# Gate and up products in steps of 512 features with the tokens as TensorE's weights, in a fp32 transformer kernel on one core

## Chip, core and metric

One Trainium2 chip, one of its cores, everything in fp32. The time of a kernel is the device time of one execution in microseconds; each run gives the time of the core. The profile is that of one more execution, which has its own time.

## What is computed

256 tokens of width 1024 go through two stacks of two layers. The first stack has, in each layer, a gated feed-forward part (ffn), an attention mixer, a cross attention to 256 memory rows, and a second ffn. The second stack has in each layer a hybrid mixer (three kinds of attention, one of them "differential") and after it, in layer 0, a dense ffn, in layer 1 eight experts. The parts that the change touches:

```python
def swiglu_ffn(x, w_gu, w_down):                    # 1024 -> 2 x 2816 -> 1024, 5 times
    gate, up = jnp.split(x @ w_gu, 2, axis=-1)
    return (jax.nn.silu(gate) * up) @ w_down
# first stack, 4 of the 5: x + 0.5 * swiglu_ffn(rms_norm(x, gain), w_gu, w_down)
# second stack, layer 0:   h = rms_norm_2(x, g_ffn) * (1 + sc2) + sh2; x + gt2 * swiglu(h, ...)
# diff_attention, per head, two softmax maps p[0], p[1] of 32-wide halves:
a = p[:, :, 0] - lam * p[:, :, 1]
y = jnp.einsum('bhqs,bshd->bqhd', a, v)             # then rms_norm, gain
# moe_swiglu: for each of 8 experts, out += combine[e] * swiglu(h, w_gate[e], w_up[e], w_down[e])
```

## The kernel before

The program is one hand-written stream of instructions for each engine; semaphores alone order the engines among one another, and every wait is written out. A plan lists the stages (norm, ffn, mixer, ...) with the running counts of every semaphore, so that each engine's code can wait for "the n-th of this kind". The feature-major activations `xT` are eight tiles of 128 features x 256 tokens.

**Weights** come through a ring of 7 slots of 1 MiB (128 x 2048 fp32), filled by SyncE (SP) in the order of use. Before each load SP waits for the semaphore value that the plan noted in `released` for that slot's last reader (`slot_free`). SP's stream is in order, so that a load that waits holds back all behind it. Gate and up weights are two loads to a step of 256 features (`L790` gate, `L793` up), each of 1 MiB.

**An ffn** takes its 2816 features in 11 steps of 256 (`j`). Step 0 is the plain product (`gate_up`, `L1250`, `L1253`). Steps 1 to 10 are Winograd's form of Strassen's product: gate and up as the two column halves, the 1024 inputs as two halves, seven products M1 to M7 in the order M1, M5, M6, M2, M3, M7, M4 instead of eight (`products`, `L1293`). A piece of weights of 128x128 is TensorE's stationary operand and 128 token columns move; one step is 112 matmul records, the results lie feature-major, 128 features x tokens. VectorE forms the sums of weights S1 to S4 of the next step in pieces of 128x512 (`weight_sums`, `L2981` to `L2989`) and the sums of products U2, U3, C12, C21, C22 (`L3037`, `L3089` to `L3114`); ScalarE copies M1, M5, C11 out of PSUM and takes tanh for silu; VectorE multiplies gate by up (`L2995`, `L2997`: a "gated pair") into `hidden`. M4 of step j is issued behind M1 of step j+1. The down product (2816 to 1024) uses the same scheme from `hidden` as it lies (`down`, `L1344`; `down_sums`, `L3021` to `L3032`).

Between the products PE does small pieces for VectorE in its last bank (`through_last_bank`, `L1313`, `L1317`), for the modulation vector whose weights POOL loads and VectorE multiplies (`ada_part`, `L2915`).

**Norm ahead of an ffn:** PE transposes x (`L1118`), VectorE writes `xT` with the gain; 1/rms per token (`rs`) is needed feature-major along the tokens, so VectorE writes a diagonal, PE multiplies it by ones (`L1136`), and VectorE multiplies the result into `xT` (`L2545`). `keep_busy` (`L1108`) are matmuls without a use, placed where PE waits.

**Hybrid mixer:** of its pairs of heads the first `ROW_PAIRS` = 4 are differential. Both maps are transposed (3 transposes a block pair each) and both multiplied by v (`L1985`, 12 records); `turn_diff` (`L1948`) transposes the finished heads at pair i=5; `turn_weights` (`L1963`) waits for the scaled maps of its pair (`p_scaled`, VectorE `L2682`).

**Experts:** their gate and up weights (`L822`, `L823`, half a MiB each, one slot together) and down weights (`L826`) go through a ring of 7 + `MORE` = 10 slots in `EXPERT_ORDER`; PE's products are `L1439` and `L1482`. Extra slots lie in buffers of earlier stages, so SP waits for `wo_done` or the like ahead of their first use.

## Time and profile before

| | us |
|---|---|
| three runs of the kernel | 2682.12, 2683.52, 2688.59 (median 2683.52) |
| the profiled execution | 2680.09 |
| its span (first to last instruction) | 2678.3 |
| PE busy | 2560.3 (96%) |
| VectorE (DVE) busy | 1311.5 (49%) |
| ScalarE (ACT) busy | 435.4 (16%) |
| GpSimd (POOL) busy | 204.2 (8%) |

Matmuls overlap their neighbours in the pipeline, so a busy PE is not a PE at its peak; how long a piece of PE's work takes is read as the distance between the starts of its first row and of the next piece's. A fp32 matmul of the code shows as two records in the counts of the trace.

### The profile page before, as it was taken

Reading aid. Unit: us, or ns where it says so; the run is one execution under the profiler, and the core shown is the slowest. Engines: PE = TensorE matmul, PEld = TensorE weight load, DVE = VectorE, ACT = ScalarE, POOL = GpSimd, SP = SyncE. Lnnn points to the kernel's source line nnn. Section 1 sums busy time; section 2 is a strip of 40 time slices with the busy share of each in tenths; the row PEclk is TensorE's granted clock in tenths of the full one; section 3 lists DMA queues with packets and bytes.
Section 4 is the critical chain, followed back from the end, with each engine's and each line's share of the span. In section 5 each row is a group of like instructions: output and inputs, shape, how many; then the busy total and the mean of one; then the engine's idle time right before and its main releaser. Section 6 shows DMA issues by size and latency. Waiting matters only on the chain.

```text
span 2678.3 us, 44222 instructions
## 1 busy us (share of the span) xinstructions
PE 2560.3 (96%) x18150; PEld 1643.6 (61%) x18150; DVE 1311.5 (49%) x2784; ACT 435.4 (16%) x1187; POOL 204.2 (8%) x330
## 2 busy tenths in 40 slices
PE   8999999999999998999999999999999899989996
PEld 8964457797599444477964649945545344634452
DVE  6887442488877955425887556664630000101002
ACT  1201252011012013321101221102310110101010
POOL 3010100000000102000001110001100000000000
PEclk9999999999999999999999999999999999999999
DMA  9684323367656743234675434544359999999997
GB/s 299 205 318 160 110 95 126 117 216 255 214 189 220 252 157 126 82 108 152 217 254 150 136 115 154 186 160 119 113 224 403 412 413 412 417 412 411 409 417 311
DMA packets 306523, 619.18 MB, mean 231 GB/s; under 512 B 15948, under 2 KB 172784, under 8 KB 306192
## 3 DMA queue, kind: packets, MB, share of 16 engines
q1 hardware_dynamic: 287088, 550.80, 55.5%
q0 software_dynamic: 19232, 65.52, 7.3%
q8 instruction: 146, 2.39, 0.3%
q14 instruction: 57, 0.47, 0.0%
HBM read 607.47 MB, written 8.79 MB: 230 GB/s over the span
## 4 chain that ended last, share of the span: by engine, by line
PE 69%; issue 10%; DVE 9%; DMA 6%; SPq 4%; ACT 1%; POOL 1%; DVEq 0%; POOLq 0%; ACTq 0%
PE psum L1293 22%; PE psum L1439 10%; PE psum L1859 6%; PE psum L1482 5%; PE psum L1344 4%; PE psum L1574 3%; DMA xn<-in_w_ada 2%; PE psum L1209 2%; PE psum L1161 2%; PE psum L1770 2%; DMA ring<-in_w_exp_up 2%; PE psum L1880 2%; SPq L822 2%; SPq L823 2%; DVE proj L2915 1%
## 5 line engine op out<-in xcount | busy, mean ns | idle before, releaser
L1439 PE MATMUL psum<-ring,xT 128*32 128x512 f32 (+3 forms) x3372 | 293.0, 494 | 17.3 <-DMA ring<-in_w_exp_up 16.7
L3409 DVE SCALAR_TENSOR_TENSOR proj<-proj,psum 128x256 f32<-128x256 f32 (+1 forms) x63 | 24.9, 395 | 555.1 <-ACT proj L2326 555.1
L1439 PEld LDWEIGHTS psum<-ring,xT 128*32 128x32 f32 x3372 | 128.0, 110 | 168.4 <-issue 111.7
L1293 PE MATMUL psum<-xT,ring 128*128 128x128 f32 x1600 | 195.0, 275 | 0.0
L1293 PEld LDWEIGHTS psum<-xT,ring 128*128 128x128 f32 x1600 | 187.7, 192 | 4.1 <-issue 3.8
L1859 PE MATMUL psum<-ring,xT 128*128 128x384 f32 (+1 forms) x448 | 156.2, 498 | 1.1 <-DVE xT L2550 1.1
L2915 DVE SCALAR_TENSOR_TENSOR proj<-xn,cols,proj 128x512 f32<-128x512 f32 x168 | 126.0, 750 | 18.3 <-DMA xn<-in_w_ada 14.3
L1574 PE MATMUL psum<-ring,memT 128*128 128x512 f32 x256 | 119.3, 605 | 8.2 <-issue 8.1
L943 POOL DMA_DIRECT2D xn<-in_w_ada x96 | 69.5, 726 | 677.0 <-DVE proj L2915 670.4
L1859 PEld LDWEIGHTS psum<-ring,xT 128*128 128x128 f32 x448 | 80.9, 190 | 61.2 <-issue 10.8
L1161 PE MATMUL psum<-ring,y 128*128 128x512 f32 x256 | 113.5, 601 | 0.7 <-ACT kTx L2086 0.7
L1482 PE MATMUL psum<-ring,proj 128*32 128x256 f32 x1872 | 104.5, 379 | 0.0
L1344 PE MATMUL psum<-ring,proj 128*128 128x512 f32 x220 | 102.6, 592 | 0.0
L1293 PE MATMUL psum<-qT,ring 128*128 128x128 f32 x800 | 98.0, 276 | 1.4 <-DVE picked L3109 1.4
L1293 PE MATMUL psum<-diff_o,ring 128*128 128x128 f32 x800 | 97.5, 275 | 0.0
L1293 PEld LDWEIGHTS psum<-qT,ring 128*128 128x128 f32 x800 | 93.3, 192 | 5.6 <-DVE picked L3109 5.6
L1293 PEld LDWEIGHTS psum<-diff_o,ring 128*128 128x128 f32 x800 | 93.3, 192 | 0.0
L1482 PEld LDWEIGHTS psum<-ring,proj 128*32 128x32 f32 x1872 | 72.9, 110 | 32.4 <-issue 6.0
L2219 ACT ACTIVATE silu<-pT 128x256 f32<-128x256 f32 x100 | 41.9, 419 | 293.1 <-DVE pT L3037 185.1
L1161 PEld LDWEIGHTS psum<-ring,y 128*128 128x128 f32 x256 | 48.6, 192 | 59.0 <-issue 57.9
L1574 PEld LDWEIGHTS psum<-ring,memT 128*128 128x128 f32 x256 | 46.1, 192 | 59.0 <-issue 58.6
L2326 ACT ACTIVATE proj<-psum 128x256 f32<-128x256 f32 (+1 forms) x63 | 23.1, 367 | 345.4 <-PE psum L1439 345.4
(528 smaller groups left out, 4197.9 us busy)
## 6 DMA issues: line engine op xcount, KB each, us to landing
ring<-in_ffn_w_gu SPq DMA_DIRECT2D x88, 1024.0 KB, 7.3
ring<-in_w_exp_down SPq DMA_DIRECT2D x62, 1024.0 KB, 16.9
xn<-in_w_ada POOLq DMA_DIRECT2D x96, 512.0 KB, 4.9
ring<-in_ffn_w_down SPq DMA_DIRECT2D x44, 1024.0 KB, 7.4
ring<-in_w_exp_gate SPq DMA_DIRECT2D x82, 512.0 KB, 11.7
ring<-in_w_exp_up SPq DMA_DIRECT2D x82, 512.0 KB, 15.6
ring<-in_w_exp_gate SPq DMA_DIRECT2D x52, 384.0 KB, 9.8
ring<-in_w_exp_up SPq DMA_DIRECT2D x52, 384.0 KB, 12.4
```

What stands on the lines that cost most here:

```text
L822: sp.dma_start(slot(u)[:, 0:4 * w], g[rows, cut]).then_inc(full, 16)
L823: sp.dma_start(slot(u)[:, 4 * w:8 * w], up[rows, cut]).then_inc(full, 16)
L943: nc.gpsimd.dma_start(ada_slot[a % 2], wv[:, 2 * q:2 * q + 2, half * 3072 + c * 512:half * 3072 + (c + 1) * 512])\
L1161: ins = mm(banks[linear_bank(st, s, b)][:, 0:w], lhsT(k, b), wt[:, k - i * ks, :], start=(k == 0), stop=(k == KT - 1))
L1209: ins = mm(banks[bank][:, :], tokens[:, k, :], w[:, k, :], start=(new and k == 0), stop=(k == 3), skip_group_check=True)
L1293: ins = mm(banks[bank][:, t * P:(t + 1) * P], weights(t)[:, k, :], tokens[:, k, :], start=(new and t == 0 and k == 0), stop=(k == 3), skip ...
L1344: ins = mm(banks[bank][:, :], tokens, weights, start=(d == 0), stop=last, skip_group_check=True)
L1439: ins = mm(o[:, :, o0:o1], xg[e % 2][:, k, 32 * g:32 * g + 32], w_[:, :, c0:c1], start=(k == 0 and n_ == 0), stop=(k == KT - 1), skip_grou ...
L1482: ins = mm(bank[32 * g:32 * g + 32, at:at + 256], tokens[:, 32 * tg:32 * tg + 32], wt[:, f, d0:d0 + 256], start=first and at == 0, stop=la ...
L1574: ins = mm(banks[7][:, :], memT[:, k, b * P:(b + 1) * P], slot(u).rearrange("p (k n) -> p k n", k=4)[:, k % 4, :], start=(k == 0), stop=(k ...
L1859: ins = mm(banks[(5, 7)[b]][:, 0:w], xT[:, k, b * P:(b + 1) * P], slot(u)[:, 0:4 * w].rearrange("p (k n) -> p k n", k=4)[:, k % 4, :], sta ...
L2915: ins = V.scalar_tensor_tensor(ada_sum, w, cols[:, 16 + k:17 + k], ada_sum, ALU.mult, ALU.add)
```

## The change

- **Gate and up, all five ffns.** Step 0 becomes `gate_up_rows`: the weights are 128x128 tiles of tokens (`xT`), 512 weight columns (256 gate, 256 up) move. The other ten steps become five of 512 features (`w` = 1 to 5, `WIDE`), in the same seven products, with sums of tokens as stationary weights and 512 feature columns moving: 4 matmuls (8 records) of 512 columns a product. A quarter of a step's weights is a unit: A11, A21, A22, A12, in this order, each loaded by two transfers of half a MiB (`L825`). Each weight sum is one instruction of 128x2048; VectorE's order around them is new.
- The hidden values now come out token-major, so PE transposes them for the down product, four 128x128 transposes for 256 features (`turn_hidden`, `L1361`), and ScalarE copies them out.
- **Norm, the four ffns of the first stack** (`how="plain"`): rs is not multiplied into `xT`; gating takes it per token (tanh of rs/2 times gate, and rs squared in the second gating instruction, as a scalar per partition). The ones product and two `keep_busy` of two matmuls go.
- **Hybrid mixer:** VectorE combines the two maps before they are transposed; transposes and value products of the differential pairs halve; `turn_diff` moves to i=8 and loses its `keep_busy`.
- **Experts:** `MORE` is 6; the three added slots lie in the buffers `cst`, `qk_rows`, `sp_rows`, one further slot (`ONCE`) is used once in `xn`.

The core of the diff:

```diff
-MORE = 3
+MORE = 6
+EXPERT_ORDER = (0, 1, 2, RING, RING + 3, RING + 2, RING + 4, RING + 5, 3, 4, 5, 6, RING + 1)
...
-        add("norm", how="early", src="x", gain=("ffn1_norm", layer), dst="xT")
+        add("norm", how="plain", src="x", gain=("ffn1_norm", layer), dst="xT")
...
-            for j in range(NSTEP):
-                done = n["tiles"] // 2 + j + 1
-                released += [("gu_done1", done), ("gu_done1", done)]
+            released += [("gu_done1", t + 1)] * 2
+            for w in range(1, WIDE + 1):
+                done = t + 1 + 2 * w
+                released += [("gu_done0", done), ("product_done", n["products"] + 7 * w - 1), ("gu_done1", done), ("gu_done0", done)]
...
+                def gate_up_unit(u, j, half):
+                    rows = slot(u).rearrange("p (k t n) -> p k t n", k=4, t=2)
                     slot_free(sp, u)
-                    sp.dma_start(slot(u).rearrange("p (k n) -> p k n", k=KT), gv[:, :, cut])\
-                        .then_inc(slot_full(u), 16)
-                    slot_free(sp, u + 1)
-                    sp.dma_start(slot(u + 1).rearrange("p (k n) -> p k n", k=KT), uv[:, :, cut])\
-                        .then_inc(slot_full(u + 1), 16)
+                    for t, wv in enumerate((gv, uv)):
+                        sp.dma_start(rows[:, :, t, :], wv[:, 4 * half:4 * half + 4, j * FSTEP:(j + 1) * FSTEP]).then_inc(slot_full(u), 16)
+                u0 = st["n0"]["units"]
+                for half in range(2):
+                    gate_up_unit(u0 + half, 0, half)
+                for w in range(1, WIDE + 1):
+                    for name in UNITS:
+                        gate_up_unit(wide_unit(u0, w, name), 2 * w - (name[1] == "1"), int(name[2]) - 1)
...
...
+                    elif n == 12:
                         sp.wait_ge(sm["wo_done"], 8)
+                    elif n == ONCE:
+                        sp.wait_ge(sm["chosen_ready"], 1)
...
+                def gate_up_rows(b):
+                    if t0:
+                        pe.wait_ge(sm[f"hid_ready{b}"], t0)
                     for k in range(KT):
+                        if k % 4 == 0:
+                            unit_in(pe, u0 + k // 4)
+                        if b == 0:
                             ready(k)
+                        ins = mm(banks[4 + b][:, :], xT[:, k, b * P:(b + 1) * P],
+                                 slot(u0 + k // 4)[:, k % 4 * 512:(k % 4 + 1) * 512], start=(k == 0), stop=(k == KT - 1))
+                    ins.then_inc(sm[f"gu_done{b}"], 1)
...
+                    if name in ("M1", "M2"):
+                        unit_in(pe, wide_unit(u0, w, "A11" if name == "M1" else "A12"))
+                    elif term is not None:
+                        pe.wait_ge(sm["weights_summed"], weighed(n0, w, term))
+                    for k in range(4):
+                        ins = mm(banks[bank][:, :], tokens[:, k, :], weights[:, k * 512:(k + 1) * 512],
+                                 start=(new and k == 0), stop=(k == 3), skip_group_check=True)
+                    if name == "M3":
+                        ins.then_inc(sm["gu_done0"], 2)
+                    elif name == "M4":
+                        ins.then_inc(sm["gu_done1"], 2)
...
+                def turn_hidden(j):
...
+                    for f in range(2):
+                        for b in range(NB):
+                            ins = nc.tensor.transpose(banks[bank][:, (NB * f + b) * P:(NB * f + b + 1) * P],
+                                                      hidden_tile[2 * j + f][:, b * P:(b + 1) * P], ident)
+                    ins.then_inc(sm["product_done"], 1)
...
+                for w in range(1, WIDE + 1):
+                    products(w, "M1")
+                    if w > 1:
+                        products(w - 1, "M4")
+                        turn_hidden(2 * w - 3)
+                    through_last_bank(2 * w - 1, 0)
+                    products(w, "M5")
+                    through_last_bank(2 * w - 1, 1)
+                    products(w, "M6")
+                    products(w, "M2")
+                    through_last_bank(2 * w, 0)
+                    turn_hidden(2 * w - 2)
+                    products(w, "M3")
+                    through_last_bank(2 * w, 1)
+                    products(w, "M7")
+                turn_hidden(NSTEP - 2)
                 for d in range(NSTEP - 2):
+                    if d == LAST_TURN:
+                        turn_hidden(NSTEP - 1)
+                    if d == 0:
+                        down(0, "P2")
+                        products(WIDE, "M4")
                     for name in DOWN_PRODUCTS:
-                        down(d, name)
-                        if d == 0 and name == "P2":
-                            products(NSTEP - 1, "M4")
+                        if d or name != "P2":
+                            down(d, name)
...
                 def turn_diff():
-                    pe.wait_ge(sm["w2_evac0"], nb * (l + 1))
-                    keep_busy(5, 2)
...
-                        if i < ROW_PAIRS:
-                            pe.wait_ge(sm[f"p_ready{b}"], w + 1)
-                        else:
-                            pe.wait_ge(sm["p_scaled"], 2 * (n0["scaled"] + i - ROW_PAIRS) + b + 1)
+                        pe.wait_ge(sm["p_scaled"], 2 * (n0["scaled"] + i) + b + 1)
                         pe.wait_ge(sm[f"pt_evac{b}"], w)
-                        for h in range(2):
+                        for h in range(1 if i < ROW_PAIRS else 2):
...
+                elif st["how"] == "plain":
...
+                    V.tensor_scalar(half_rs, rs, 0.5, None, ALU.mult)
+                    V.tensor_tensor(square_rs, rs, rs, ALU.mult).then_inc(sm["diag_ready"], 1)
...
+                    if i < ROW_PAIRS:
+                        link(V.tensor_scalar(rden[:, :, 1], rden[:, :, 1], stat[:, 14:15], None, ALU.mult))
+                        for b in range(NB):
+                            p = p_sb[b][:, :, 0:(b + 1) * P]
+                            link(V.tensor_scalar(p[:, 0, :], p[:, 0, :], rden[:, b, 0:1], None, ALU.mult))
+                            V.scalar_tensor_tensor(p[:, 0, :], p[:, 1, :], rden[:, b, 1:2], p[:, 0, :], ALU.mult, ALU.add)\
+                                .then_inc(sm["p_scaled"], 1)
+                        return
...
+                            ins = V.tensor_tensor(S1, A21, A22, ALU.add)
...
+                            ins = V.tensor_tensor(S2, S1, A11, ALU.subtract)
+                        elif name == "S3":
+                            ins = V.tensor_tensor(A21, A11, A21, ALU.subtract)
+                        else:
+                            unit_in(dve, units["A12"])
+                            if w > 1:
+                                dve.wait_ge(sm["gu_done0"], t0 + 1 + 2 * (w - 1))
+                            dve.wait_ge(sm["weights_summed"], weighed(n0, w, "S2"))
+                            ins = V.tensor_tensor(S4, A12, S2, ALU.subtract)
+                        ins.then_inc(sm["weights_summed"], 1)
...
+                for w in range(1, WIDE + 1):
...
+                    if w > 1:
+                        second_column(w - 1, 1)
+                        last_sum(w - 1)
+                        second_column(w - 1, 0)
...
+                        ada_part(st, 2 * w - 1)
...
+                    V.tensor_tensor(c12_rows, banks[Z][:, :], m1_copy[w % 2], ALU.add).then_inc(sm["part_summed"], 1)
+                    if w < WIDE:
+                        weight_sums(w + 1, ("S1",))
+                    first_column(w, 0)
...
+                    if w < WIDE:
+                        weight_sums(w + 1, ("S2",))
...
+                    dve.wait_ge(sm["gu_done0"], t0 + 1 + 2 * w)
+                    V.tensor_tensor(c12_rows, banks[Y][:, :], c12_rows, ALU.add).then_inc(sm["part_summed"], 1)
+                    if w < WIDE:
+                        weight_sums(w + 1, ("S3", "S4"))
+                    else:
                         down_sums(0)
...
+                    first_column(w, 1)
+                    dve.wait_ge(sm["product_done"], produced(n0, w, "M7"))
+                    if w > 1:
+                        dve.wait_ge(sm["hid_ready1"], hidden_number(n0, w - 1, 1))
+                    V.tensor_tensor(second_rows, banks[Z][:, :], m1_copy[w % 2], ALU.add).then_inc(sm["part_summed"], 1)
+                    if "ada" in st:
+                        ada_part(st, 2 * w)
...
+                    V.tensor_tensor(second_rows, second_rows, m5_copy, ALU.add).then_inc(sm["part_summed"], 1)
```

In that code `c12_rows` is U2 and then C12, `second_rows` is U3 and then C22, `last_sum` is C21, `first_column` and `second_column` are the gated pairs (two instructions each), `from_last_bank` takes what `through_last_bank` made. The three places below show it in the streams.

**VectorE, one ffn step from U2 on, before.** (`kTx`, `s_sb`, `ring` hold weight sums, `picked` the token-side sums, `pT` values for gating, `proj` the hidden values.)

```order
L3089 TENSOR_TENSOR picked<-psum,kTt 128x256 [waits product_done,part_copied,part_summed]
L3037 TENSOR_TENSOR pT<-psum,picked 128x2x128 [waits gu_done1]
L2984 TENSOR_TENSOR kTx<-kTx,ring1 128x512 [waits weights_summed]
L2984 TENSOR_TENSOR kTx<-kTx,ring2 128x512 [waits weights_summed]
L2995 SCALAR_TENSOR_TENSOR silu1<-silu1,pT 128x256 [waits silu_done1,part_summed]
L2997 TENSOR_TENSOR proj<-pT,silu1 128x256 [waits gated1]
L3102 TENSOR_TENSOR pT<-psum,picked 128x2x128 [waits gu_done0,part_summed]
L2987 TENSOR_TENSOR s_sb0<-ring1,kTx 128x512 [waits weights_summed]
L2987 TENSOR_TENSOR s_sb1<-ring2,kTx 128x512 [waits weights_summed]
L2995 SCALAR_TENSOR_TENSOR silu0<-silu0,pT 128x256 [waits silu_done0,part_summed,part_copied]
L2997 TENSOR_TENSOR proj<-pT,silu0 128x256 [waits gated0]
L3109 TENSOR_TENSOR picked<-psum,kTt 128x256 [waits product_done]
```

VectorE in the changed kernel, first wide step of the first ffn, from `first_column(w, 0)` to U3:

```order
L3105 SCALAR_TENSOR_TENSOR silu0<-silu0,psum 128x256 [waits silu_done0]
L3108 SCALAR_TENSOR_TENSOR proj<-silu0,stat,psum 128x2x128 [waits gated0]
L3089 TENSOR_TENSOR vx<-kTx,ring3 128x2048 [waits weights_summed,product_done,ring_full3]
L3228 TENSOR_TENSOR pT<-psum,pT 128x512 [waits gu_done0,part_summed]
L3091 TENSOR_TENSOR ring4<-ring3,ring4 128x2048
L3097 TENSOR_TENSOR sp_rows<-ring6,vx 128x2048 [waits weights_summed,gu_done0,ring_full6]
L3105 SCALAR_TENSOR_TENSOR silu0<-silu0,pT 128x256 [waits silu_done0,part_summed]
L3108 SCALAR_TENSOR_TENSOR proj<-silu0,stat,pT 128x2x128 [waits gated0]
L3237 TENSOR_TENSOR hid<-psum,picked 128x512 [waits hid_ready1,product_done]
```

Before, no sum of weights between C12 (`L3102`) and U3 (`L3109`) waits for a slot of the ring; now S4 (`L3097`) does (`ring_full6`), and the second gated pair and U3 (`L3237`) stand behind it.

**SyncE, loads of gate and up, before** (a row is a transfer of 1 MiB; both loads of a step wait for the same count of M4):

```order
L790 DMA ring5<-in_ffn1_w_gu 128x8x256 [waits gu_done1]
L793 DMA ring6<-in_ffn1_w_gu 128x8x256 [waits gu_done1]
```

and in the changed kernel, the four units of one wide step, A11, A21, A22, A12:

```order
L825 DMA ring3<-in_ffn1_w_gu 128x4x256 [waits product_done]
L825 DMA ring3<-in_ffn1_w_gu 128x4x256
L825 DMA ring4<-in_ffn1_w_gu 128x4x256 [waits gu_done1]
L825 DMA ring4<-in_ffn1_w_gu 128x4x256
L825 DMA ring5<-in_ffn1_w_gu 128x4x256 [waits gu_done0]
L825 DMA ring5<-in_ffn1_w_gu 128x4x256
L825 DMA ring6<-in_ffn1_w_gu 128x4x256 [waits gu_done0]
L825 DMA ring6<-in_ffn1_w_gu 128x4x256
```

The plan gives A12 of step w+1 the slot of A11 of step w, and its load the wait for `gu_done0`, which counts M3 of step w.

**PE in the changed kernel**, M1 and M4 and then M2, a turn and so on (`x3` are further rows of the same form):

```order
L1335 MATMUL psum<-sp_rows,xT 128x512 [waits weights_summed,part_copied]
L1335 MATMUL psum<-sp_rows,xT 128x512 x3
L1335 MATMUL psum<-ring0,diff_o 128x512 [waits weights_summed,part_summed]
L1335 MATMUL psum<-ring0,diff_o 128x512 x3
L1335 MATMUL psum<-ring3,xT 128x512 [waits ring_full3,hid_ready0]
L1335 MATMUL psum<-ring3,xT 128x512 x3
L1335 MATMUL psum<-ring1,qk_rows 128x512 [waits part_summed]
L1335 MATMUL psum<-ring1,qk_rows 128x512 x3
L1361 MATMUL psum<-cst,proj 128x128 [waits part_copied,hid_ready0]
L1361 MATMUL psum<-cst,proj 128x128 x3
```

`ring3` begins M1 of step w+1, and M4 of step w (`ring1`) stands behind it with a wait for `part_summed`, the count that U3 of step w raises. Before, M4 of step j stood behind M1 of step j+1 with the same wait.

## Rows read from the trace of the kernel before

Rows of a timeline: start and length in us, engine, line, operation, out<-in, shapes, count, and in brackets how long the engine had been idle and what ended it. A row that bundles several matmuls ends a little after the next row starts.

**Rows 1.** The page: busy time of the engines; DMA share in 40 slices.

```profile
PE 2560.3 (96%) x18150; PEld 1643.6 (61%) x18150; DVE 1311.5 (49%) x2784; ACT 435.4 (16%) x1187; POOL 204.2 (8%) x330
...
DMA  9684323367656743234675434544359999999997
```

**Rows 2.** Chain that ended last, one Strassen step: start, us, what.

```profile
82.78 12.51 PE psum L1293 x112
95.28 0.44 PE psum L1313 x4
```

**Rows 3.** Timeline, PE, down product of 512 columns.

```profile
163.19 1.88 PE L1344 MATMUL psum<-kTx,s_sb 128*128 128x512 f32 x4
164.90 1.02 PE L1344 MATMUL psum<-ring,s_sb 128*128 128x512 f32 x2
```

**Rows 4.** Timeline, PE, norm, first step and first product of an ffn.

```profile
498.46 2.09 PE L1118 MATMUL psum<-cst,x 128*128 128x128 f32 x16
...
503.73 3.69 PE L1250 MATMUL psum<-xT,ring 128*128 128x256 f32 x16 [0.27 <-DVE xT L2545]
...
517.62 1.61 PE L1293 MATMUL psum<-xT,ring 128*128 128x128 f32 x13
```

**Rows 5.** Timeline, PE's last product of a step and the load that it releases.

```profile
44.23 1.95 PE L1293 MATMUL psum<-xT,ring 128*128 128x128 f32 x16
44.43 0.54 SPq L793 DMA_DIRECT2D ring<-in_ffn_w_gu  x1
```

**Rows 6.** The loads of `L793`, all of them.

```profile
DMA to landing us min/median/max: 5.0/5.2/13.7
```

**Rows 7.** DMA issues, SyncE, 1960.5 to 1961.3 us: KB each, us to landing.

```profile
ring<-in_w_exp_gate SPq DMA_DIRECT2D x1, 512.0 KB, 3.5
ring<-in_w_exp_up SPq DMA_DIRECT2D x1, 512.0 KB, 4.4
```

**Rows 8.** Groups of VectorE by form: busy us, mean ns, idle before.

```profile
L2989 DVE TENSOR_TENSOR ring<-ring 128x512 f32<-128x512 f32 x100 | 64.1, 682 | 0.0
L2997 DVE TENSOR_TENSOR proj<-pT,silu 128x256 f32<-128x256 f32 x100 | 42.5, 425 | 3.4
L3102 DVE TENSOR_TENSOR pT<-psum,picked 128x256 f32<-128x256 f32 x50 | 21.2, 423 | 53.2 <-PE psum L1293 53.2
```

**Rows 9.** Timeline, VectorE's `down_sums`, C12, and PE's M4 of the last step.

```profile
149.74 0.28 DVE L3021 TENSOR_TENSOR p_sb<-proj 128x128 f32<-128x128 f32 x1
...
152.96 0.41 DVE L3102 TENSOR_TENSOR pT<-psum,picked 128x256 f32<-128x256 f32 x1
...
155.29 2.05 PE L1293 MATMUL psum<-qT,ring 128*128 128x128 f32 x16 [0.29 <-DVE picked L3109]
```

**Rows 10.** Timeline, PE, norm of another stage, which uses no rs row.

```profile
228.40 1.15 PE L1118 MATMUL psum<-cst,x 128*128 128x128 f32 x8 [0.77 <-DVE x L3052]
230.28 1.10 PE L1209 MATMUL psum<-ring,xT 128*128 128x512 f32 x2 [0.74 <-DVE xT L2570]
```

**Rows 11.** Timeline, hybrid mixer: value products, `keep_busy`, `turn_diff`, scaled maps.

```profile
1498.95 1.45 PE L1985 MATMUL psum<-proj,pT 128*128 128x64 f32 x12
...
1545.81 1.88 PE L1108 MATMUL psum<-cst 128*128 128x512 f32 x4
1548.70 0.66 PE L1948 MATMUL psum<-cst,y 128*128 128x128 f32 x4 [1.00 <-DVE y L2715]
...
1548.77 1.03 DVE L2682 TENSOR_TENSOR p_sb<-p_sb,rden 128x256 f32<-128x256 f32 x2
```

**Rows 12.** Stretches in the experts and the end: us, engines' busy, PEclk, DMA share, GB/s.

```profile
2200.00:2300.00 100.00, 100.00 (x1416) 57.66 (x1411) 8.11 (x21) 11.46 (x32) 1.62 (x3) 1.00 1.03 413
2600.00:2678.00 78.00, 51.25 (x504) 18.12 (x496) 14.51 (x22) 5.66 (x17) 5.14 (x6) 0.94 0.81 328
```

**Rows 13.** Timeline, SyncE's expert loads, and PE late in the last expert.

```profile
1960.61 0.33 SPq L822 DMA_DIRECT2D ring<-in_w_exp_gate  x1
...
2616.30 1.92 PE L1439 MATMUL psum<-kTx,xT 128*32 128x512 f32 x16 [3.08 <-DMA kTx<-in_w_exp_up]
```

More of the change, by code:

```diff
@@ L257, in block1 @@
         xattn()
-        add("norm", how="early", src="x", gain=("ffn2_norm", layer), dst="xT")
+        add("norm", how="plain", src="x", gain=("ffn2_norm", layer), dst="xT")
         add("ffn", w=("ffn2", layer), out="half", ada=2 * layer + 1)
@@ L278, in make_plan @@
     add("final")
-    n = dict(products=0, copies=0, sums=0, weighed=0, norm=0, early=0, chunks=0, units=0, tiles=0, pieces=0, pairs=1, staged=1, soft=1, scaled=0, stick=1, xupd=0, prep=0,
+    n = dict(diag=0, products=0, copies=0, sums=0, weighed=0, norm=0, early=0, chunks=0, units=0, tiles=0, pieces=0, pairs=1, staged=1, soft=1, scaled=0, stick=1, xupd=0, prep=0,
              roots=0, squares=0)
@@ L300, in make_plan @@
             n["early"] += how == "early"
+            st["diag"] = n["diag"]
+            n["diag"] += how in ("early", "plain")
         st["root_of"] = root
@@ L504, in build @@
         shift_sum = lamv[:, 1, 0, 0:NEXP]
-        logits, first, second, count = (s_sb[0][:, 0, 16 * n:16 * n + 16].rearrange("p (b e) -> p b e", b=NB) for n in range(4))
-        sel = p_sb[0][:, :, 0:P]
-        selT = qT[:, 0, :]
+        routing = pT_rows[:, :, :, :].rearrange("p h b s -> p (h b s)")
+        sel = routing[:, 0:S].rearrange("p (b s) -> p b s", b=NB)
+        selT = routing[:, S:2 * S]
+        order_tmp = routing[:, 2 * S:3 * S]
+        logits, first, second, count, part = (routing[:, 3 * S + 16 * n:3 * S + 16 * n + 16].rearrange("p (b e) -> p b e", b=NB)
+                                              for n in range(5))
+        shift = routing[:, 3 * S + 80:3 * S + 80 + NEXP]
         mem = y
@@ new lines, in gate_up_rows, with products @@
+                    ins.then_inc(sm[f"gu_done{b}"], 1)
+                n0 = st["n0"]
+                def products(w, name):
+                    X, Y, Z = ((4, 6, 5), (1, 3, 2))[w % 2]
+                    whole = {part: slot(wide_unit(u0, w, part)) for part in UNITS}
+                    bank, new, weights, tokens = {
+                        "M1": (X, True, whole["A11"], B11), "M2": (X, False, whole["A12"], B21), "M5": (Y, True, S1, T1),
+                        "M3": (Y, False, S4, B22), "M6": (Z, True, S2, T2), "M7": (Z, False, whole["A21"], T3),
+                        "M4": (Z, False, whole["A22"], T4)}[name]
+                    if name in ("M1", "M6") and w == 2:
@@ L1283, in products @@
                     elif name == "M4":
[L1284 removed]
+                        pe.wait_ge(sm["part_summed"], summed(n0, w, "U3"))
                     term = {"M5": "S1", "M6": "S2", "M3": "S4", "M7": "S3"}.get(name)
[L1287 to L1294 removed]
@@ L2008, in hybrid @@
                         scores(i + 1)
+                    if i == DIFF_AT:
+                        turn_diff()
                     beside(i, 1)
```

563 lines of the change are left out of this document (282 added, 281 removed).

## The prediction, made before the changed kernel ran

> **What bounds the kernel now.** I read the page first. PE is busy 96% of the span, VectorE 49%, ScalarE 16%; in the 40 slices DMA is the full resource only in the last quarter [rows 1]. So up to about 1900 us a piece of PE's work is worth its whole length, and another engine's work costs something only where PE waits for it. From there on it is turned round: between 2200 and 2300 us the DMA share is 1.03 at 413 GB/s, and late in the last expert PE waits 3.08 us for weights [rows 12, 13]; there only bytes, or the time at which their transfers start, count. The chain of waits through a feed-forward step is then nothing but PE: 12.51 us for the 112 records of a step of 256 features, next piece at 95.28 [rows 2]. PE has no stall there to lose, so a gain must come from fewer or shorter matmuls, and any new stall is a loss in full.
>
> **Sum, term by term.** Against the profiled execution (2680.1 us, span 2678.3), which lies 3.4 us under the median of the runs shown.
>
> *1. Columns.* A step of 256 costs 12.51 us, two of them 25.02 [rows 2]. The new product moves 512 columns, the form of the down product, whose four records take from 163.19 to 164.90, 0.4275 us each [rows 3]. Seven products of 8 records are 23.94 us. Saved: 1.08 us a wide step, 25 such steps in five ffns: **-27.0**. The plain step 0 runs from 503.73 to 517.62, 13.89 us [rows 4]; 32 records of 0.4275 are 13.68: **-1.0** for five.
>
> *2. Transposes.* Four records of 128 columns take 0.44 us [rows 2]. Each of the 11 pieces of 256 hidden features now needs four of them on PE: 11 x 0.44 x 5 = **+24.2**. ScalarE's copies behind them have an engine with 84% idle, and no product waits for one directly. Terms 1 and 2 together are nearly nothing: what wide products save, the turned layout takes back.
>
> *3. The wait for S4.* This decides. The plan puts the unit A12 of step w+1 into the slot of A11 of step w, whose load waits for M3 of step w. VectorE's S4 of step w+1 reads A12, and behind it in VectorE's order stand the second gated pair and U3 of step w; M4 of step w on PE waits for U3. Count from the end of M3: the load is issued 0.20 us after the product that frees it (44.23 to 44.43 [rows 5]). A unit of 1 MiB that has its slot alone lands after 5.2 us in the median, 5.0 at best [rows 6]; as two halves issued one behind the other the nearest row is 0.37 + 4.4 = 4.8 (the second half is issued 0.37 behind the first) [rows 7, 13]. I take 5.2, because the modulation weights that POOL loads and units released just before share the rings in most ffns. S4 is 128x2048; the widest sum in the trace is 128x512 at 0.682 us, and 128x256 takes 0.423 [rows 8]. That slope gives 0.682 + 6 x 0.259 = 2.24; four times the 512 form would be 2.73. A gated pair is 2 x 0.43, U3 at 128x512 0.68 [rows 8]. Sum 0.20 + 5.2 + 2.24 + 0.86 + 0.68 = 9.18 us. PE meanwhile has M7 and M1 of the next step, 16 x 0.4275 = 6.84. M4 waits 2.34 us. Steps w = 1 to 4 of each ffn have a next step, so 20 such waits: **+46.8**. Bounds: landing 4.8 gives 1.94 and +39; S4 at 2.73 gives 2.83 and +57; nothing at all is rival A. A wait here is not made up later, since PE has no other stall that it could shorten.
>
> On the landing the Trainium skill, DMA: Bandwidth & Descriptors, section "Anatomy of one DMA — SWDGE (gpsimd) path", has a rule: about 2.0 us and then the bytes at 436 GB/s. For 1 MiB that is 4.4 us, an estimate by that page, where [rows 6] has 5.0 at least. By it the wait would be 1.5 us, the term +31 and the result about 2692 against the median. On S4, VectorE: DVE Perf Modes, section on the TRN2 errata, has (N+151)/0.96 ns for a fp32 sum, 2.29 us at 2048 columns, which the slope of the rows (2.24) comes near; it would add 1 us to the sum.
>
> *4. The end of the wide steps.* In the last one VectorE has C12, `down_sums(0)` and the first gated pair before `turn_hidden(9)` can run. `down_sums` takes from 149.74 to 152.96, 3.22 us [rows 9]; with C12 at 0.68, the pair at 0.86 and 0.2 of signalling 5.0 us, against one product M7 of 3.42: PE waits 1.6, where the last M4 waited 0.29 [rows 9]. **+6.5** for five ffns (0 to +10, if the order behind it absorbs it, or if `turn_hidden(9)` also waits for a copy).
>
> *5. Norm.* PE's transposes start at 498.46, take 2.09, and the first product starts at 503.73 [rows 4]: with the ones product and `keep_busy` in between. Without rs the first product needs only `xT` of the first feature tile, 0.74 us behind the transposes in the stage that has this form already [rows 10]: 498.46 + 2.09 + 0.74 = 501.29, 2.4 us sooner. The first ffn of all gains nothing, as its weights are still landing; three times 2.4: **-7.2**. The two small instructions that make rs/2 and its square lie on VectorE under the 13.7 us of step 0; if that cover were gone they would cost about 0.4 us a norm.
>
> *6. Hybrid mixer.* A differential pair loses 3 transposes (0.33 us by [rows 2]) and half of the value products (1.3 us between starts, 1.45 in [rows 11], so 0.65): 0.98 x 4 = 3.9 a layer. At `turn_diff`, `keep_busy` and a wait of 1.00 stand between 1545.81 and 1548.70, 2.7 us that go. But the scaled maps of pair 5 are ready at 1548.77 + 1.03 = 1549.80 only [rows 11], and `turn_weights(5)` now comes sooner and waits for them: 1.5 given back. 5.1 a layer, **-10.2** for two. VectorE's combination of the maps replaces the separate scaling; if it becomes what the early pairs wait for, the gain shrinks to -4; if nothing is given back, -14.
>
> *7. Experts.* From the first expert on DMA sets the pace. A unit of 1 MiB at 413 GB/s is 2.54 us [rows 12]. Three slots more let three more units be moved before PE's first expert product: 3 x 2.54 = **-7.6**. Bounds 0 (their buffers come free too late, or the ring was not what held the stream) and -10.2 with the slot in `xn`.
>
> Sum: -27.0 - 1.0 + 24.2 + 46.8 + 6.5 - 7.2 - 10.2 - 7.6 = **+24.5**, so 2704.6 by the profiled execution and **2708** against the median. A difference under 0.3% (8 us) can't be told from none.
>
> **Rivals.**
>
> *A, the unit is in time (the other side).* If A12 lands within 5.2 - 2.34 = 2.9 us of M3's end, S4 costs PE nothing, and the sum is 24.5 - 46.8 = -22.3: 2661 against the median, faster. For it: without the landing, the rest (0.20 of issue, S4, pair, U3, 4.0 us) fits well under 6.84. Against it: the fastest 1 MiB in the trace took 5.0, half a MiB alone 3.5 [rows 6, 7]. The point from which it decides: waits under 0.7 us each make the kernel faster by over 0.3%. Chance 0.13.
>
> *B, the landing is short but not short enough.* The two halves go over the rings together with nothing beside them, and the unit lands 4.0 to 4.5 us after its issue (half a MiB took 3.5 [rows 7], and another half MiB at 413 GB/s is 1.3 more [rows 12], from its own start 0.37 later). Waits of 1.1 to 1.6 us, +23 to +33 in place of 46.8, so 2684 to 2694. This is the rival that the DMA page above stands for. Chance 0.14, most of it within 0.3%.
>
> *C, the clock.* Where PE had 51.25 us busy of 78, its granted clock in the mean was 0.94, not 1.00 [rows 12], which is a part of the stretch at 1.2 GHz. If each of the 20 waits puts half a product behind it (four records, 1.7 us) at 1.2 GHz instead of 2.4, that adds 1.7 us each, +34: 2742. Against it: short waits of 0.3 to 1 us in [rows 4, 9, 11] are not seen in the clock of the page. Chance 0.06.
>
> *My forecast*, waits of 1.9 to 2.8 us and the joined changes near their sizes: 0.67. Its own range is 2696 to 2722: landing -8, S4 +10, joined changes 6 either way, taken together by squares on the low side about 12 and on the high side 14.
>
> **Numbers.** 2708. Leaving out A (0.13) and C (0.06) gives 2680 to 2726. Faster by over 0.3% (below 2675.5): A, and a little of B with larger joined gains, 0.15. Within 0.3%: most of B, 0.12. Slower: 0.73.
>
> **What would show it.** In the changed kernel's trace each M4 of w = 1 to 4 should stand behind an idle time of PE of about 2.3 us that ends with U3 on VectorE, and VectorE's S4 behind an idle time that ends with a DMA of the ring; seven products should take 24 us, a turn 0.44, S4 2.2 to 2.3. First product of an ffn 2.8 us after the first transpose. Experts: the first product sees more units landed, the end comes 7.6 us sooner against the start of the experts. Wrong it would be if the idle time ahead of M4 is below 1.2 us (then the change is no loss), if the turns hide in waits that are there anyway, or if products of 512 columns run at other than 0.43 us a record.

## The result, and the profile of the changed kernel

| | before | changed |
|---|---|---|
| median of the runs of this comparison, us | 2682.88 | 2729.84 |
| lowest to highest | 2682.12 to 2688.59 | 2725.39 to 2732.47 |
| ratio (95% interval) | | 1.0169 (1.0148 to 1.0189) |
| span of the profiled execution | 2678.3 | 2730.3 |

The changed kernel is 47 us slower, where 25 were forecast; 2729.84 lies 4 us above the range. The wait that was forecast is there, in its place and at its size; PE's clock behind it, which the sum had at nothing, is not as forecast.

The first lines of the changed kernel's page, the engines and three of its groups (count, busy us, mean ns, idle time before and what ended it):

```profile
PE 2561.2 (94%) x13902; PEld 1271.9 (47%) x13902; DVE 1297.8 (48%) x2391; ACT 438.8 (16%) x1142; POOL 204.3 (7%) x330
...
L1335 PE MATMUL psum<-ring,qk_rows 128*128 128x512 f32 x200 | 106.9, 684 | 47.7 <-DVE hid L3237 47.7
...
L1335 PE MATMUL psum<-ring,diff_o 128*128 128x512 f32 x200 | 90.0, 593 | 0.7 <-DVE pT L3218 0.7
...
L3097 DVE TENSOR_TENSOR sp_rows<-ring,vx 128x2048 f32<-128x2048 f32 x25 | 57.3, 2291 | 38.8 <-DMA ring<-in_ffn_w_gu 30.1
```

PE is busy for as long as before [rows 1], with a quarter fewer matmuls. `ring,qk_rows` is M4, `ring,diff_o` is M7, the same number of matmuls of the same shape. (In the listing of PE's stream ahead of the prediction the first two products are therefore M3, from `sp_rows`, and M7; M1 and M4 follow.) Two things are to be seen. Ahead of M4 PE idles 47.7 us in all, and what ends it is U3 (`L3237`); VectorE's S4 (`L3097`) in its turn waits for a load. And M4 itself is busy 106.9 us where M7 takes 90.0: the same work at a mean of 684 ns in place of 593.

The chain that ended last, between 74.6 and 88 us, goes through one such wait:

```profile
75.06 0.02 issue
75.08 0.37 SPq L825
75.45 0.04 issue
75.49 4.79 DMA ring<-in_ffn_w_gu
80.28 0.02 issue
80.31 0.03 DVE sp_rows L3097
80.34 2.17 issue
82.52 0.43 DVE silu L3105
...
83.37 0.69 DVE hid L3237
84.07 0.04 issue
84.11 3.70 PE psum L1335 x8
```

M3 ends at about 75.06, SyncE issues the load, it has landed at 80.28, S4 runs, then the gated pair, then U3, and M4 starts at 84.11: 9.05 us, where the prediction had 9.18. PE's own timeline behind two waits of the same length (start, length, and in brackets the idle time):

```profile
555.30 5.40 PE L1335 MATMUL psum<-ring,qk_rows 128*128 128x512 f32 x8 [2.09 <-DVE hid L3237]
560.53 0.60 PE L1361 MATMUL psum<-cst,proj 128*128 128x128 f32 x4
...
584.25 3.70 PE L1335 MATMUL psum<-ring,qk_rows 128*128 128x512 f32 x8 [2.08 <-DVE hid L3237]
```

The first M4 takes until the next piece starts at 560.53, 5.23 us, the second 3.54. The windows of the two (length, busy and counts of PE, weight load, VectorE, ScalarE, GpSimd, then PEclk, DMA share, GB/s) say why:

```profile
584.00:588.00 4.00, 3.75 (x10) 1.79 (x11) 3.13 (x7) 0.99 (x2) 0.72 (x1) 1.00 0.14 24
...
555.00:561.00 6.00, 5.70 (x13) 2.63 (x14) 3.52 (x7) 0.99 (x2) 0.72 (x1) 0.72 0.29 87
```

Granted clock 1.00 (2.4 GHz) behind one wait, and a mean of 0.72, so 1.2 GHz for about half of the stretch, behind the other. Over the whole execution:

```profile
core 0: 2730.3 us, clock 0.987
```

and before:

```profile
core 0: 2678.3 us, clock 0.995
```

Span times clock is 2694.8 against 2664.9: of the 52 us between the two profiled executions about 30 are work and waits at full clock, 22 are the clock. The stretches at 1.2 GHz in the two traces say where: none stands in an ffn before the change, ten do after it (nine behind an M4, one behind a turn that had waited 2.45 us), 1.7 us lost in each; the rest stands in other stages.

By the starts of the first rows of each stage on PE, in us:

| | before | changed | difference |
|---|---|---|---|
| first transposes to first product, four ffns of the first stack | 21.7 | 13.1 | -8.6 |
| five ffns, first product to the next stage | 1064.7 | 1137.4 | +72.7 |
| two hybrid mixers | 292.6 | 281.2 | -11.4 |
| experts, first transposes to the end of the span | 714.4 | 713.5 | -0.9 |
| all else | 584.9 | 585.1 | +0.2 |

### The profile page after: what moved, and what is told of

Its sections match the earlier page's. It is cut to its first block, busy times and chain, and to the rows that moved or that the text cites. A ratio compares the mean times of both kernels' runs of the same rounds, so it can differ in the third digit from the quotient of the medians.

```text
span 2730.3 us, 35231 instructions
## 1 busy us (share of the span) xinstructions
PE 2561.2 (94%) x13902; PEld 1271.9 (47%) x13902; DVE 1297.8 (48%) x2391; ACT 438.8 (16%) x1142; POOL 204.3 (7%) x330
## 4 chain that ended last, share of the span: by engine, by line
PE 68%; DVE 9%; issue 9%; DMA 8%; SPq 4%; POOL 1%; ACT 0%; DVEq 0%; POOLq 0%; ACTq 0%
PE psum L1335 16%; PE psum L1515 11%; PE psum L1410 6%; PE psum L1935 6%; PE psum L1558 5%; PE psum L1212 4%; PE psum L1650 3%; DMA ring<-in_ffn_w_gu 3%; DMA xn<-in_w_ada 2%; PE psum L1260 2%; PE psum L1299 2%; PE psum L1846 2%; PE psum L1960 2%; SPq L873 2%; SPq L874 1%
## 5 line engine op out<-in xcount | busy, mean ns | idle before, releaser
L1515 PE MATMUL psum<-ring,xT 128*32 128x512 f32 (+3 forms) x2588 | 230.9, 503 | 15.6 <-DMA ring<-in_w_exp_up 15.0
L1335 PE MATMUL psum<-ring,xT 128*128 128x512 f32 x400 | 179.8, 592 | 0.0
L1335 PE MATMUL psum<-ring,qk_rows 128*128 128x512 f32 x200 | 106.9, 684 | 47.7 <-DVE hid L3237 47.7
L1335 PEld LDWEIGHTS psum<-ring,xT 128*128 128x128 f32 x400 | 76.0, 190 | 95.7 <-issue 95.4
L1935 PEld LDWEIGHTS psum<-ring,xT 128*128 128x128 f32 x448 | 80.9, 190 | 61.2 <-issue 10.8
L1410 PE MATMUL psum<-ring,sp_rows 128*128 128x512 f32 x220 | 105.2, 592 | 0.0
L1335 PE MATMUL psum<-ring,diff_o 128*128 128x512 f32 x200 | 90.0, 593 | 0.7 <-DVE pT L3218 0.7
L1335 PE MATMUL psum<-sp_rows,xT 128*128 128x512 f32 x200 | 90.0, 592 | 0.0
L1335 PE MATMUL psum<-kTx,qk_rows 128*128 128x512 f32 x200 | 89.9, 592 | 0.0
L1335 PE MATMUL psum<-vx,qk_rows 128*128 128x512 f32 x200 | 89.9, 592 | 0.0
L3097 DVE TENSOR_TENSOR sp_rows<-ring,vx 128x2048 f32<-128x2048 f32 x25 | 57.3, 2291 | 38.8 <-DMA ring<-in_ffn_w_gu 30.1
```

What stands on the lines that cost most here:

```text
L1335: ins = mm(banks[bank][:, :], tokens[:, k, :], weights[:, k * 512:(k + 1) * 512], start=(new and k == 0), stop=(k == 3), skip_group_check= ...
L1410: ins = mm(banks[bank][:, :], tokens, weights, start=(d == 0), stop=last, skip_group_check=True)
L1515: ins = mm(o[:, :, o0:o1], xg[e % 2][:, k, 32 * g:32 * g + 32], w_[:, :, c0:c1], start=(k == 0 and n_ == 0), stop=(k == KT - 1), skip_grou ...
L1935: ins = mm(banks[(5, 7)[b]][:, 0:w], xT[:, k, b * P:(b + 1) * P], slot(u)[:, 0:4 * w].rearrange("p (k n) -> p k n", k=4)[:, k % 4, :], sta ...
L3097: ins = V.tensor_tensor(S4, A12, S2, ALU.subtract)
```

## Experiments

The ratios are those of each run to the kernel before on the same chip.

**1. S4 behind U3.** Nothing else is moved.

```diff
-                        weight_sums(w + 1, ("S3", "S4"))
+                        weight_sums(w + 1, ("S3",))
                     else:
                         down_sums(0)
                     first_column(w, 1)
...
                     V.tensor_tensor(second_rows, banks[Z][:, :], m1_copy[w % 2], ALU.add).then_inc(sm["part_summed"], 1)
+                    if w < WIDE:
+                        weight_sums(w + 1, ("S4",))
```

> The changed kernel with one instruction moved: VectorE forms S4 of step w+1 behind U3 of step w, not ahead of the second gated pair. Theory (the loss is PE's wait for U3 behind S4's wait for the load of A12, and the half-speed stretches of PE that follow such waits): the 20 waits ahead of M4 (51.7 us of stall in the changed kernel's trace) go and the half-speed work of the ffn stages (some 17 us more than before) goes with them: 2662 us, 0.8% below the kernel before, mean granted clock back near 0.994. Rival 1 (the lower clock belongs to the wide products themselves or is chance): only the stall goes, 2680, clock stays at 0.987. Rival 2 (S4 behind U3 makes S4 or C22 late for PE): new waits ahead of M3 or a turn, 2700 or more.

Measured: 2668.47 us against 2687.8, ratio 0.9926 (0.9909 to 0.9943). The changed kernel's 1.0169 has become 0.9926, 2.4% or 65 us for one instruction's place. The groups of PE by line, the same two as above:

```profile
L1335 PE MATMUL psum<-ring,qk_rows 128*128 128x512 f32 x200 | 91.8, 603 | 4.4 <-DVE hid L3237 4.4
L1335 PE MATMUL psum<-ring,diff_o 128*128 128x512 f32 x200 | 90.0, 593 | 0.2 <-DVE pT L3218 0.2
```

47.7 us of waiting are 4.4, and M4 takes nearly what M7 takes: two stretches at 1.2 GHz are left in the ffns in place of ten. In the profiled executions, 60 us apart, 43 are waiting, 14 the clock and 2 M4's start behind a wait (3.54 us from start to start, without one 3.43). The theory's 2662 stood in ratio for 0.992; rivals 1 and 2 (2680, over 2700) are out. S4 now ends 12.6 to 16.0 us ahead of its own product M3, so that the load's landing costs nothing there.

**2. The wait filled, not removed.** The changed kernel with two matmuls at the start of M1 that its first own matmul overwrites.

```diff
+                    if name == "M1" and w > 1:
+                        for _ in range(2):
+                            mm(banks[bank][:, :], tokens[:, 0, :], weights[:, 0:512], start=True, stop=True, skip_group_check=True)
                     for k in range(4):
```

> The changed kernel with two more matmuls of 512 columns (four records, 1.7 us) at the start of M1 of steps 2 to 5, which M1's own first matmul overwrites: PE is busy for 1.7 of the 2.3 us that it waits ahead of M4; nothing else moves. Theory (PE's idle time ahead of M4 is what lowers the clock): the idle time falls from 47.7 to about 14 us, the waits end when they did, and the half-speed stretches go: about 15 us less than the changed kernel, 2714. Rival (the clock falls with the wide products or by chance): no change, 2730, clock 0.987. If the added work is not hidden after all: up to +34, 2764.

Measured: 2717.22, ratio 1.0110 (1.0094 to 1.0127), 0.6% or 16 us less than the changed kernel, with 34 us of matmuls added. Its groups by line (M4 and M7; the line is 1338 here):

```profile
L1338 PE MATMUL psum<-ring,qk_rows 128*128 128x512 f32 x200 | 93.7, 612 | 14.2 <-DVE hid L3240 14.2
L1338 PE MATMUL psum<-ring,diff_o 128*128 128x512 f32 x200 | 90.0, 593 | 0.3 <-DVE pT L3221 0.3
```

The idle time is 14.2 as expected, and M4's busy time fell from 106.9 to 93.7. M4 still waits for the same U3, and starts 8.8 to 9.7 us after M3's end in 18 of the 20 cases, as it did in 19 of the 20 without the filling, so nothing became shorter but the stretches at 1.2 GHz: one is left in the ffns in place of ten, 15 us. The mean clock of the profiled execution is 0.995, of the other three 0.991 to 0.993, against 0.987 to 0.990 of the changed kernel. Work that is thrown away made the kernel faster. This shows that PE's idle time ahead of M4 is what lowers the clock behind it; that it is the wide products themselves is out.

**3. Every turn made twice.**

```diff
-                    for f in range(2):
+                    for f in (0, 1, 0, 1):
                         for b in range(NB):
                             ins = nc.tensor.transpose(banks[bank][:, (NB * f + b) * P:(NB * f + b + 1) * P],
```

> The changed kernel with every transpose of hidden values made twice (eight for 256 features in place of four; the second writes the same values again). Theory (the turns lie wholly on PE's path, 0.44 us each): +24 us, 2754. Rival (a part hides in waits that are there anyway): the turns of w = 1 to 4 that stand behind the waits and those ahead of M3 delay nothing, below +12, under 2742.

Measured: 2756.38, ratio 1.0250 (1.0233 to 1.0267), so 0.8% or 22 us above the changed kernel (15 to 29 by the two intervals), against +24 of the theory and under +12 of the rival. The waits ahead of M4 stayed, 45.6 us in place of 47.7. The turns lie on PE's path with nearly their whole length.

**4. down_sums(0) behind U3 as well.** On top of experiment 1, `down_sums(0)` of the last wide step goes behind U3 too.

> As the kernel with S4 behind U3, and in the last wide step down_sums(0) also behind the gated pair and U3. Theory (the stall of about 1.5 us ahead of the turn of hidden step 9 is VectorE's order): 1.5 x 5 = 7 us less than with S4 moved alone, 2655 us. Rival (the first down products, which need down_sums(0), wait instead): no difference from S4 moved alone, 2662.

Measured: 2677.75, ratio 0.9957 (0.9941 to 0.9974): 9 us slower than experiment 1, by neither expectation. PE's waits of this run (us in total, times, longest) and its timeline with ScalarE's:

```profile
PE psum L1410 <- ACT proj L2302: 10.6, 5, 2.4
```

```profile
647.61 0.68 DVE L3244 TENSOR_TENSOR hid<-hid,pT 128x512 f32<-128x512 f32 x1
...
648.33 0.51 ACT L2293 ACTIVATE silu<-hid,stat 128x256 f32<-128x256 f32 x1 [8.12 <-DVE hid L3244]
648.75 0.58 ACT L2302 ACTIVATE proj<-psum 128x512 f32<-128x512 f32 x1
...
649.47 2.05 PE L1410 MATMUL psum<-ring,proj 128*128 128x512 f32 x2 [2.43 <-ACT proj L2302]
```

The turn is made in time now, but its copy (`L2302`) stands on ScalarE behind a tanh (`L2293`) that waits for C22 (`L3244`), and C22 had come behind `down_sums(0)`. The stall went from PE's turn to the copy of its result, for which a down product waits: four times 2.43 us and once 0.89, 3 us more than the turns' 7.3 us in experiment 1. And three of the four longer waits are followed by a stretch at 1.2 GHz, 5 us together, where the turns' waits of 1.5 us had none behind them. By this the clock is the larger part of the 9 us.

**5. The copy ahead of that tanh.** On top of experiment 4:

```diff
-                    second_tanh(WIDE, 1)
                     turned_copy(NSTEP - 2)
+                    second_tanh(WIDE, 1)
```

> The kernel with S4 and down_sums(0) both behind U3, and on ScalarE the copy of turn 9 ahead of the tanh of the last step's second column, which waits for C22 that now comes behind down_sums(0). Theory (the wait of 10.6 us for that copy ahead of the first down product is ScalarE's order alone): that wait goes, and with it the stall of 1.5 us ahead of the turn: 7 us less than the kernel with S4 behind U3 alone, 0.990 of the kernel before. Rival (down_sums(0) is itself late for the products that use it): a new wait ahead of them, no better than S4 alone.

Measured beside experiment 1 once more:

> The kernel with S4 behind U3 once more, as the base that the three others of this call are compared with on the same chip: 0.9926 of the kernel before, as in the first call.

The base came out at 2669.24, ratio 0.9936 (0.9922 to 0.9949), this kernel at 2666.23, 0.9928 (0.9915 to 0.9942), and in a third comparison (experiment 8) again at 0.9928 (0.9913 to 0.9942, 2665.10 us). The wait for the copy is gone from the list of PE's waits, so the cause found in experiment 4 is shown. The gain over experiment 1 is 3 us, with intervals that overlap, not 7: pieces of the modulation vector on PE now wait for VectorE instead (7.1 us in six waits; 2.2 in four in the base):

```profile
PE psum L1382 <- DVE proj L3020: 7.1, 6, 3.5
```

**6. The norm as before the change.** On experiment 1, `how="early"` again for the four ffns. The gating then takes no rs, as before the change. This kernel does not compute the function: part of its values are wrong, for a reason that no run shows, so it serves for its time alone.

> The kernel with S4 behind U3, and the norm of the first stack's four ffns as before the change (rs multiplied into xT, with the ones product and keep_busy). Theory (each of the three later norms is 2.4 us shorter by the change, the first is bound by its weights' landing): 7 us more than its base. Rival (the time between transposes and the first product is taken by something else, such as VectorE's sums of weights): no difference.

Measured: 2673.30, ratio 0.9951 (0.9938 to 0.9965), 4 us above its base (0.9936); the intervals overlap, and by them the difference lies between -1 and +9. The total does not settle the term, but the traces do. The changed kernel, from the transposes to the first product of the second ffn:

```profile
512.00 2.10 PE L1169 MATMUL psum<-cst,x 128*128 128x128 f32 x16
514.76 1.53 PE L1299 MATMUL psum<-ring,xT 128*128 128x512 f32 x3 [0.67 <-DVE xT L2649]
```

These are 2.76 us. For the three later norms the stretch is 5.26, 5.33 and 5.03 us in this kernel and 2.78, 2.85 and 2.76 in its base: 7.2 us, the theory's 7.

**7. The experts' ring as before the change.** On experiment 1, 10 slots.

```diff
-EXPERT_ORDER = (0, 1, 2, RING, RING + 3, RING + 2, RING + 4, RING + 5, 3, 4, 5, 6, RING + 1)
+EXPERT_ORDER = (0, 1, 2, RING, 3, 4, 5, 6, RING + 1, RING + 2)
...
-        if n == ONCE:
-            return ONCE
-        at = EXPERT_ORDER[(n - (n > ONCE)) % EXPERT_RING]
+        at = EXPERT_ORDER[n % 10]
```

> The kernel with S4 behind U3, and the experts' ring with its 10 slots, their order and their waits as before the change. My term of the prediction: 7.6 us more than its base. Rival from the changed kernel's trace (from the first expert product to the end it was 4.1 us shorter, and two half-speed stretches fell into the routing ahead of it by chance): 4 us more. Rival 2 (the ring's length is not what holds the stream): no difference.

Measured: 2669.87, ratio 0.9939 (0.9925 to 0.9953) against 0.9936 of its base. No difference that can be measured: by the two intervals it lies between -4 and +6 us, so the 7.6 us of the prediction are out, and the 4 us of the rival are not.

**8. The hybrid part alone on the kernel before,** and beside it the kernel of experiment 5 again.

```diff
-                        for h in range(2):
+                        for h in range(1 if i < ROW_PAIRS else 2):
...
-                        for h in range(2):
-                            for t in range(b + 1):
-                                ins = mm(banks[6][:, b * P + h * 64:b * P + (h + 1) * 64], pT[h][:, b + t, :], value_rows(t, h),
-                                         start=(t == 0), stop=(t == b))
+                        for t in range(b + 1):
+                            ins = mm(banks[6][:, b * 64:(b + 1) * 64], pT[0][:, b + t, :], value_rows(t, 0), start=(t == 0), stop=(t == b))
```

> The kernel before with the hybrid mixer's part of the change alone (maps combined on VectorE before they are transposed, turn_diff at i=8, its order beside the output projection). My term: 10.2 us; the stage lengths of the changed kernel's trace say 5.8 and 5.6: 11.4 us less than the kernel before, ratio 0.9958. Rival (a part of it belongs to what the wide steps and the ring changed around it): 0.998 or more. If the ratio is the same as that of the kernel with S4 late (0.993), the cured wide steps are worth nothing.

> The kernel with S4 and down_sums(0) behind U3 and the copy of turn 9 ahead of the tanh, once more, beside the kernel before with the hybrid part alone on the same chip: 0.9928 of the kernel before again, so 8 us under the one with the hybrid part alone. This is what 25 wide steps, the norm and the ring are worth once the waits are gone: by their terms -27.0 - 1.0 + 24.2 - 7.2 and at most -1 for the ring, -12 us together. Rival: they are worth nothing and the two kernels are within 3 us.

Measured: 0.9959 (0.9943 to 0.9975), 2673.13 against 2684.34, so 11 us for the hybrid part, with 10.2 predicted; and 0.9928 for the kernel of experiment 5, 8 us less. Of the 19 us by which the repaired kernel beats the one before, more than half has nothing to do with gate and up. What is left, 8 us by two medians whose intervals just part (0.9942 and 0.9943), is the norm, the ring and 25 wide steps with their turns. The two traces (spans 4.5 us apart) say which: the stretch between transposes and first product is 8.4 us shorter in four ffns, but the five ffns themselves take 1069.4 us (1071.8 in experiment 5's own trace) against 1063.4. In these executions the wide steps, cured of their wait, still cost 6 us, and the norm gains more than that; no run has the wide steps alone.

## Why the prediction was right or wrong

By its own terms, from both traces:

*Columns (-27.0, -1.0).* A product without a wait takes 3.43 us from start to start, so each of its eight records 0.429 and not 0.4275, which over 1400 records is 2 us. Right within 3 us.

*Turns (+24.2).* Right, and borne out by doubling (+22).

*The wait for S4 (+46.8).* Right in its mechanism, place, number and size: 47.7 us in 20 waits. The landing was 5.2 us from issue (75.08 to 80.28 in the chain), the row's median and not the shorter value. S4 took 2291 ns, 2% above the slope of [rows 8]. Rival A and rival B are out.

The Trainium skill's fit for a transfer (DMA: Bandwidth & Descriptors, "Anatomy of one DMA — SWDGE (gpsimd) path", an estimate of 4.4 us for 1 MiB) is given for loads that GpSimd issues; for this one, issued by SyncE, it would have been short by 0.8 us. The formula for a fp32 sum that the Trainium skill has in VectorE: DVE Perf Modes, section on the TRN2 errata, gives 2291 ns at 2048 columns, and the trace agrees with 2291.

One thing neither the prediction nor a run looked at: by the code the load of A12 waits longer than it has to. On PE only M1 reads A11, and from w = 2 on VectorE has read it for S2 and S3 before M5 can start; yet its slot is released by M3, which ends three products and a turn after M5. Releasing it with M5 would let the load start some 10 us sooner (an estimate, 3 x 3.43 + 0.44, not tried), and S4 could stay where it is.

*The clock.* This is the step that failed. The sum had nothing for it: the prediction priced it as rival C, 1.7 us for each wait and +34, gave it a chance of 0.06, and argued against it from waits of 0.3 to 1 us that leave the clock at 1.00. Those waits were shorter than the new ones by a factor of two and more, and said nothing about 2.3 us. The trace of before had better rows. Apart from the one at its start PE has four waits over 2 us in it, and three of them are followed by a stretch at 1.2 GHz. One is this, with the window behind it:

```profile
337.93 1.47 PE L1659 MATMUL psum<-cst,p_sb 128*128 128x128 f32 x5 [2.56 <-DVE p_sb L2828]
```

```profile
338.00:348.50 10.50, 9.09 (x34) 5.63 (x35) 1.23 (x3) 4.56 (x9) 0.00 (x0) 0.51 0.36 139
```

The granted clock there is 0.51. The changed kernel shows 1.7 us lost behind 9 of the 20 waits (M4 took 5.0 to 5.2 us from start to start there, 3.54 behind the others): of the 106.9 - 90.0 = 17 us that M4 is busy longer than M7, 15 are the clock and 2 its start behind a wait. A tenth fall, ahead of a turn, makes the clock's part in the ffns 17 us. Experiments 1 and 2 take it away, one by removing the wait, one by filling it. All 9 stood behind an idle time of 1.96 us or more, but so did nine others at full clock, one of them behind 2.76: here such an idle time made a fall possible, not certain. Without these 17 us the measured 2729.84 would be 2713, inside the range.

The ffns as a whole: their terms sum to +49.5 (columns, turns, the wait, the end), measured are +72.7. The 23 us between them are the clock 17, the end of the wide steps 5 (below), the records 2, M4's start behind a wait 2 and the wait itself 1, less 4 by which the pieces of the modulation vector wait less for VectorE than before (1.5 us in place of 5.7).

*The range.* Its sum by squares is off: 8 and 6 give 10, 10 and 6 give 12, where it has 12 and 14. The range that was stated, 2680 to 2726, leaves rival C out by intent and so has no room for the clock.

*The end of the wide steps (+6.5).* Right in place, too small. PE's waits ahead of turns by line in the changed kernel:

```profile
PE psum L1361 <- DVE proj L3108: 6.0, 4, 1.5
PE psum L1361 <- DVE diff_o L3044: 5.2, 4, 2.4
```

The first row (and 1.4 more in a row of the dense ffn) is the turn of step 9, 1.5 us each, where the prediction had 1.6. The second was not seen: the last turn uses the bank of the modulation vector's pieces and waits until VectorE has read it. 12.6 us in all where the sum had 8.

*Norm (-7.2).* Right: the three stretches are 7.3 us shorter in the changed kernel, and experiment 6 gives 7.2 back. The first ffn's is 1.3 us shorter too.

*Hybrid mixer (-10.2).* 11 us by experiment 8; the stages are 11.4 us shorter in the changed kernel.

*Experts (-7.6).* Wrong by nearly its whole size in the total: 0.9 us from the stage's first transposes to the end. The chain of the changed kernel, ahead of the first expert product, shows what took a part back:

```profile
2019.35 5.28 PE psum L2134 x32
...
2030.90 5.42 PE psum L1464 x32
2036.32 0.03 issue
```

and before:

```profile
1966.48 3.87 PE psum L2061 x32
...
1976.39 3.80 PE psum L1388 x32
1980.19 0.02 issue
```

The same 32 small matmuls of the routing take 1.4 and 1.6 us longer, both in part at the lower clock, and the first expert product comes 21.0 us into the stage in place of 17.8. From there to the end it is 4.1 us shorter. That is less than three units' time. The rate between 2100 and 2600 us is 410 GB/s against 413, which over 500 us is 3.6 us (53 us later, at the same place of the stage, it is 411). First the changed kernel, then before:

```profile
2100.00:2600.00 500.00, 479.62 (x6090) 236.70 (x6083) 43.48 (x114) 48.03 (x134) 9.62 (x18) 1.00 1.03 410
```

```profile
2100.00:2600.00 500.00, 476.78 (x6094) 237.79 (x6086) 43.45 (x114) 49.70 (x139) 8.54 (x17) 1.00 1.03 413
```

The second 32 take 5.4 us in the traces of all ten experiments' runs, with the old ring and without the wide steps too; what all of them share is the hybrid part. The first 32 range from 3.6 to 5.0 there. Why the routing meets the lower clock, whether the one trace of before is the exception by chance, and whether the rate belongs to the added slots stays open.

## What to carry to other kernels

When a wait is predicted on the engine that is the bound, price the clock with it: here moving one line took away 43 us of idle time and 65 us of the kernel's, and filling the idle time with thrown-away matmuls gave 16 back. Look in the trace for waits as long as the forecast one, not for shorter ones. Before an instruction that waits for a load is placed, look at what is queued behind it on its engine: S4 was needed more than 12 us later, the two things behind it at once, and one moved line was worth 2.4%. Follow a moved wait through the in-order engines: `down_sums(0)` out of PE's way stood in ScalarE's, and cost more there. And when several changes are joined, measure the parts: by the traces the wide steps that this change is named for gained nothing even when cured.

## What the runs showed of the hardware

PE's granted clock fell to 1.2 GHz behind 9 of 20 idle times of 1.6 to 4.6 us between dense stretches of products of 512 columns (none of the 9 under 1.96 us). With the same gaps filled to 0.6 us or less in 16 of the 20, one fall was left among the 20, behind a gap of 2.85 us; a gap of 2.52 had none. Each fall cost 1.7 us. In experiment 4 three of four waits of 2.43 us ahead of a down product had a fall, too.
